# Moving weight sums, a transpose and a tail between engines in a decoder layer on eight cores

## The reference

```python
hcat = x @ w_in                          # B, C, h (512 each) | q, k, v, g (512 each)
y_conv = B * causal_short_conv(C * h, conv_w)            # 3 taps, depthwise
q, k = rotary(q), rotary(k) * 128 ** -0.5
o = chunkwise_retention(q, k, v)         # 4 heads of 128, decay, running state
y_ret = silu(g) * head_group_norm(o)
mix = concat([y_conv, y_ret]) @ w_out
x = layer_norm(alpha * x + mix)
ff = square(relu(x @ w_ff1)) @ w_ff2     # 1024 -> 4096 -> 1024
ple = sigmoid(x @ w_ple_gate) * (p @ w_ple_proj)
x = layer_norm(alpha * x + ff + ple)
```

## Time and profile before

| | us |
|---|---|
| median of 6 runs | 953.4 (946.37 to 958.29) |
| profiled execution | 950.21 |
| span of its slowest core (core 0) | 948.7 |
| spans of the other cores | 894.7 to 948.6 |
| PE busy on core 0 | 783.1 (83%) |
| DVE busy | 579.7 (61%) |
| ACT busy | 226.3 (24%) |
| POOL busy | 162.7 (17%) |

### The profile page before, as it was taken

How to read it: one execution, slowest core, us unless ns; L and a number is a source line. 1 busy time by engine, 2 the same in 40 slices (tenths; PEclk the granted TensorE clock), 3 DMA queues, 4 the chain that set the end, 5 groups by cost and what they waited for, 6 DMA issues and landing times.

```text
span 948.7 us, 12219 instructions; the slowest of 8 cores (894.7 to 948.7 us)
## 1 busy us (share of the span) xinstructions
PE 783.1 (83%) x3864; PEld 362.2 (38%) x3864; DVE 579.7 (61%) x832; ACT 226.3 (24%) x456; POOL 162.7 (17%) x208
## 2 busy tenths in 40 slices
PE   4999958788878973899999999800699999999980
PEld 1444424444434421344444444300244444444430
DVE  4558756559987692566447773200376766657697
ACT  2222234443454201344332000000033333200000
POOL 8000235434545311001000000000011110000011
PEclk9999989999999986899999999955799999999995
DMA  9992665687456996957321345995547553234112
GB/s 128 163 212 39 103 152 124 140 179 160 114 122 133 252 191 135 242 126 162 114 89 45 133 170 96 146 56 42 109 97 172 163 187 120 90 133 168 55 66 111
DMA packets 54207, 124.20 MB, mean 131 GB/s; under 512 B 16000, under 2 KB 32512, under 8 KB 47232
## 3 DMA queue, kind: packets, MB, share of 16 engines
q0 software_dynamic: 13248, 51.91, 31.8%
q1 hardware_dynamic: 39744, 69.42, 27.1%
q10 hardware_dynamic: 1152, 2.10, 0.6%
HBM read 133.37 MB, written 30.41 MB: 173 GB/s over the span
## 4 chain that ended last, share of the span: by engine, by line
PE 57%; DMA 13%; DVE 10%; issue 5%; SPq 5%; POOL 4%; another core or an unknown queue 4%; ACT 2%; DVEq 0%; POOLq 0%; ACTq 0%
PE ps L178 56%; SPq L220 5%; DVE xacc L196 3%; DMA ycat<-s_x 3%; DMA s_x<-x1b_54 3%; DMA stg_122<-w_ff 2%; DMA xT_56<-xT 2%; DMA s_op<-stg_121 1%; DMA stg_121<-w_ff 1%; DVE xacc L185 1%; POOL st_51 L185 1%; DVE lnst L987 1%; DVE stg_121 L185 1%; ACT sqj L207 1%
## 5 line engine op out<-in xcount | busy, mean ns | idle before, releaser
L185 DVE TENSOR_TENSOR xacc<-xacc,ps 128x512 f32<-128x512 f32 x96 | 63.7, 684 | 129.5 <-PE ps L178 127.8
L178 PE MATMUL ps<-ycat,ring_106 128*128 128x512 bf16 x256 | 60.5, 400 | 19.1 <-DMA ycat<-s_x 17.0
L207 ACT ACTIVATE tR_129<-ps 128x512 f32<-128x512 f32 x43 | 25.6, 596 | 199.6 <-PE ps L178 193.0
L185 POOL TENSOR_TENSOR lnst<-lnst,neghalf 128x1 f32<-128x1 f32 x32 | 23.8, 745 | 268.9 <-DVE lnst L189 268.8
L178 PE MATMUL ps<-ring_104,ycat 128*128 128x512 bf16 x256 | 60.7, 387 | 5.3 <-DVE xtmp L196 5.2
L178 PE MATMUL ps<-ring_105,hT 128*128 128x512 bf16 x64 | 15.8, 409 | 58.1 <-DMA ring_105<-s_op 58.1
L178 PE MATMUL ps<-ring_105,ycat 128*128 128x512 bf16 x256 | 60.2, 384 | 0.5 <-DVE xtmp L196 0.5
L185 DVE TENSOR_TENSOR hT<-ps,tR_127 128x512 bf16<-128x512 f32 x43 | 29.6, 689 | 48.4 <-ACT tR_127 L207 47.3
L178 PE MATMUL ps<-ycat,ring_107 128*128 128x512 bf16 x256 | 55.9, 379 | 0.0
L178 PE MATMUL ps<-ring_109,ycat 128*128 128x512 bf16 x224 | 51.9, 379 | 0.0
L178 PE MATMUL ps<-ring_108,ycat 128*128 128x512 bf16 x224 | 51.9, 379 | 0.0
(11 more groups left out here) (262 smaller groups left out, 1419.9 us busy)
## 6 DMA issues: line engine op xcount, KB each, us to landing
s_op<-stg_121 SPq DMA_DIRECT2D x8, 896.0 KB, 6.2
s_op<-stg_122 SPq DMA_DIRECT2D x8, 896.0 KB, 9.3
ring_104<-s_op SPq DMA_DIRECT2D x6, 1024.0 KB, 4.8
ring_105<-s_op SPq DMA_DIRECT2D x6, 1024.0 KB, 5.0
stg_121<-w_ff POOLq DMA_DIRECT2D x8, 512.0 KB, 6.6
stg_122<-w_ff POOLq DMA_DIRECT2D x8, 512.0 KB, 5.6
xtmp<-x SPq DMA_DIRECT2D x8, 512.0 KB, 12.9
ring_106<-w_ff POOLq DMA_DIRECT2D x4, 1024.0 KB, 11.5
```

Source lines behind the costliest of these rows:

```text
L178: self.P.op("pe", lambda e: e.matmul(out, lhsT=lhsT, rhs=rhs, start=start, stop=stop, skip_group_check=skip), reads, writes)
L185: self.P.op(eng, lambda e: e.tensor_tensor(out=out, in0=in0, in1=in1, op=op), reads, writes)
L207: self.P.op("act", lambda e: e.activation(out=out, in_=in_, func=func, **kw), reads, writes)
```

## The change

- **Staging.** Five buffers in place of two. Pieces 0 to 5 are loaded right after the other weights; their sums run on GpSimd, written ahead of the convolution. Their buffers 0 and 1 lie where the retention's `qr`, `kr`, `vb`, `qkT`, `PT` and `Sb` will be, buffer 2 on the rotary scratch. Pieces 6 to 13 stay in the retention on DVE, loaded at even t and summed at odd t, in buffers 3 and 4. Pieces 14 and 15 are loaded after the loop and summed on GpSimd in the projection. The output projection's slabs are asked for at t = 3 in place of before the loop.
- **`s_op`** is laid out by piece: the store has runs of 7 KB, a slab load runs of 1 KB in place of 8 KB.
- **Tile 1** is transposed by PE, with an ACT cast and copy for each block, in the projection's blocks 12 to 15; the LayerNorms of tiles 2 and 3 both go to the first ff1.
- **Transposing loads** of tiles 2 and 3 are issued by ACT; the second of a tile writes a name of its own (`x1T`), which the matmuls of ff1 and gate read as well.
- **Second half's order** is M1, M2, M5, M3, M4, M6, M7; the sums for M6 and M7 run on GpSimd, written ahead of M5 and of M3.
- **Tail.** For all blocks but block 3: scale and shift to mean 0 on ACT, the weight on DVE, the bias on GpSimd, one output DMA on SP's queue.

```diff
-ORDER = (("M1", "M2", "M5", "M6", "M7", "M3", "M4"), ("M1", "M3", "M2", "M4", "M5", "M6", "M7"))
+ORDER = (("M1", "M2", "M5", "M6", "M7", "M3", "M4"), ("M1", "M2", "M5", "M3", "M4", "M6", "M7"))
...
-    s_op = nc.dram_tensor("s_op", [7, 2, 128, 8, 512], BF16).ap()
+    s_op = nc.dram_tensor("s_op", [16, 128, 7, 512], BF16).ap()
...
-    stg = [at("stg%d" % i, [128, 7, 512], BF16, (o_wc + 16 * KB, o_tR)[i], ("stg", i))
-           for i in range(2)]
+    stg = [at("stg%d" % i, [128, 7, 512], BF16, off, ("stg", i))
+           for i, off in enumerate((o_rb, o_rb + 7 * KB, o_rt, o_tR, o_wc + 16 * KB))]
+    STG = [0, 1, 2, 3, 0, 1] + [3, 4] * 5
...
-                    h.dma("sp", ring[i][:], s_op[PRODS[nm][0], g], ("ringh", i),
-                          [("s_op", g * 8 + c) for c in range(8)],
+                    h.dma("sp", ring[i][:],
+                          s_op[g * 8:g * 8 + 8, :, PRODS[nm][0], :].rearrange("c p n -> p c n"),
+                          ("ringh", i), [("s_op", g * 8 + c) for c in range(8)],
                           [("ring", i)])
...
+        def gen_piece(c, eng):
+            i = STG[c]
+            t, r = stg[i], [("stg", i)]
+            h.tt(eng, t[:, 4, :], t[:, 0, :], t[:, 3, :], ALU.add, r, r)
             yield
+            h.tt(eng, t[:, 5:7, :], t[:, 1:3, :][:, ::-1, :], t[:, 0:4:3, :], ALU.subtract, r, r)
             yield
+            h.tt(eng, t[:, 1:3, :], t[:, 1:3, :], t[:, 0:4:3, :], ALU.add, r, r)
+            h.dma("sp", s_op[c], t[:], ("stgst", i), r, [("s_op", c)])
             yield
...
+        for c in range(4):
+            piece_load(c)
+        for c in range(6):
+            for _ in gen_piece(c, "pool"):
+                pass
+            if c >= 2 and c + 2 < 6:
+                piece_load(c + 2)
+
         conv((0, 0), by_piece=True)
...
-        piece_load(0)
-        prefetch(2)
-        piece_load(1)
...
-                h.dma("sp", ycat[:, a, 4 * k:4 * k + 4, :], s_x1[tt, :, k * 512:(k + 1) * 512],
-                      ("x1tr", k), [("s_x1", 4 * tt + b) for b in range(4)], ycr(a),
-                      transpose=True)
+                h.dma("act", ycat[:, a, 4 * k:4 * k + 4, :], s_x1[tt, :, k * 512:(k + 1) * 512],
+                      ("x1tr", a, k), [("s_x1", 4 * tt + b) for b in range(4)],
+                      ycr(a) if k == 0 else [("x1T", a)], transpose=True)
...
-            if t < NB:
-                pieces.add(gen_piece(t))
+            if t % 2 == 0 and t < NB:
+                piece_load(6 + t // 2)
+            elif t < NB:
+                pieces.add(gen_piece(6 + t // 2, "dve"))
...
-            if t >= 1:
-                piece_load(t + 1)
...
+            if t == 3:
+                prefetch(2)
...
         pieces.flush()
-        bg.add(gen_norm1(1))
-        prefetch(6)
+        piece_load(14)
+        piece_load(15)
+        for b in range(4, 8):
+            chains.append(gen_ln1(b))
+            bg.add(chains[b])
+        prefetch(5)
         for b in range(8, 16):
             for hf in range(2):
                 mix_part(b, hf, wo[hf][0], wo[hf][1], next_bank())
                 bg.step(3)
             if b == 11:
-                bg.flush()
-                x1_load_T(1)
-                bg.add(gen_norm1(2))
-        bg.add(gen_norm1(3))
+                for c in (14, 15):
+                    for _ in gen_piece(c, "pool"):
+                        pass
+            if b >= 12:
+                bg.until(chains[b - 8])
+                x1_cast(b - 8)
+                x1_transpose(b - 8)
+        for tt in (2, 3):
+            bg.add(gen_norm1(tt))
...
+                if n == 0:
                     bg.add_first(hsum("M2"))
-                if m in nxt:
-                    bg.add_first(hsum(nxt[m]))
+                if m == "M2":
+                    bg.add_first(hsum("M5"))
+                if m == "M5" and last:
+                    for _ in hsum("M6", "pool"):
+                        pass
+                if m == "M3" and last:
+                    for _ in hsum("M7", "pool"):
+                        pass
+                if m in ("M5", "M6") and not last:
+                    bg.add_first(hsum({"M5": "M6", "M6": "M7"}[m]))
...
+            if b != 3:
+                nb = lnst[:, b, 15:16]
+                h.stt(nb, mv[:, 0:1], -1.0, rstd, ALU.mult, ALU.mult, [rl, ("rstd", b)], [("nb", b)])
+                h.act(buf, buf, AF.Identity, [rb, ("rstd", b), ("nb", b)], [rb], scale=rstd, bias=nb)
+                yield
+                h.tt("dve", buf, buf, lnt[2][:], ALU.mult, [rb, "ln2w"], [rb])
+                yield
+                h.tt("pool", buf, buf, lnt[3][:], ALU.add, [rb, "ln2b"], [rb])
+                h.dma("sp", out[ob_ * 128:(ob_ + 1) * 128, :], buf, ("outl", b, 0), [rb],
+                      [("out", ob_, 0)])
```

More of the change, by code:

```diff
@@ L460, in piece_load @@
             if c < 16:
[L461 to L465, removed]
+                i = STG[c]
+                cast(stg[i][:, 0:4, :], w_ff2[c], ("stg", i), ("stg", i))
+        def gen_piece(c, eng):
+            i = STG[c]
+            t, r = stg[i], [("stg", i)]
+            h.tt(eng, t[:, 4, :], t[:, 0, :], t[:, 3, :], ALU.add, r, r)
             yield
-            h.tt("dve", t[:, 5:7, :], t[:, 1:3, :][:, ::-1, :], t[:, 0:4:3, :], ALU.subtract, r, r)
+            h.tt(eng, t[:, 5:7, :], t[:, 1:3, :][:, ::-1, :], t[:, 0:4:3, :], ALU.subtract, r, r)
             yield
-            h.tt("dve", t[:, 1:3, :], t[:, 1:3, :], t[:, 0:4:3, :], ALU.add, r, r)
-            h.dma("sp", s_op[:, c // 8, :, c % 8, :].rearrange("m p n -> p m n"), t[:],
-                  ("stgst", c % 2), r, [("s_op", c)])
+            h.tt(eng, t[:, 1:3, :], t[:, 1:3, :], t[:, 0:4:3, :], ALU.add, r, r)
+            h.dma("sp", s_op[c], t[:], ("stgst", i), r, [("s_op", c)])
             yield
@@ L878, in phase_ff1 @@
                             h.mm(ps[bank][:], slab[:, kc, f * 128:(f + 1) * 128],
-                                 ycat[:, a, kc, :], kc == 0, kc == 7, [rs] + ycr(a), [RP[bank]])
+                                 ycat[:, a, kc, :], kc == 0, kc == 7,
+                                 [rs, ("x1T", a)] + ycr(a), [RP[bank]])
                         i = rn[0] % 3
@@ L898, in phase_gate @@
                         h.mm(ps[bank][:], ycat[:, b // 4, kc, ck(b)], slab[:, kc, :],
-                             kc == 0, kc == 7, ycr(b // 4) + [rs], [RP[bank]])
+                             kc == 0, kc == 7, ycr(b // 4) + [rs, ("x1T", b // 4)], [RP[bank]])
                     h.act(sg[i][:], ps[bank][:], AF.Sigmoid, [RP[bank]], [("sg", i)])
@@ L922, in hv, with hsum @@
                     [("hT", fh * 16 + c, a) for c in range(c0, c1)])
-        def hsum(m):
+        def hsum(m, eng="dve"):
             ba, bb, sign = PRODS[m][1]
@@ L928, in hsum @@
                 (va, ra_), (vb_, rb_) = hv(ba, c, c + 4), hv(bb, c, c + 4)
-                h.tt("dve", dst[:, c:c + 4, :], va, vb_, ALU.add if sign > 0 else ALU.subtract,
+                h.tt(eng, dst[:, c:c + 4, :], va, vb_, ALU.add if sign > 0 else ALU.subtract,
                      ra_ + rb_, rd)
@@ L949, in phase_ff2 @@
             for n, m in enumerate(order):
-                nxt = {"M2": "M5", "M5": "M6", "M6": "M7"} if not last else {
-                    "M3": "M2", "M2": "M5", "M4": "M6", "M6": "M7"}
-                if n == 0 and not last:
+                if n == 0:
                     bg.add_first(hsum("M2"))
-                if m in nxt:
-                    bg.add_first(hsum(nxt[m]))
+                if m == "M2":
[8 more added lines that the diff above has]
+                    bg.add_first(hsum({"M5": "M6", "M6": "M7"}[m]))
                 two = [None, None]
@@ L974, in phase_ff2 @@
                             ff2_add(4 * a + p, hf, bank, sign)
-                        if last and m == "M5":
+                        if last and m == "M3":
                             last_stats(p, 1)
+                        if last and m == "M4":
+                            last_stats(4 + p, 0)
                         if last and m == "M6":
-                            last_stats(4 + p, 0)
                             bg.add(gen_last(4 + p, 1))
@@ L1001, in gen_last @@
             yield
+            ob_ = 8 + b
+            if b != 3:
[8 more added lines that the diff above has]
+                      [("out", ob_, 0)])
+                outs.append(("out", ob_, 0))
+                yield
+                return
             halves = [(buf[:, k * 512:(k + 1) * 512], (rb, "half", k)) for k in range(2)]
@@ L1007, in gen_last @@
                 yield
-            ob_ = 8 + b
             for k in range(2):
```

## The result

The kernel after takes 928.1 us (median of 10 runs, 921.6 to 935.5), the kernel before 954.05 in the same comparison (20 runs); the ratio is 0.973, its 95% interval 0.969 to 0.977. It is faster, by 26 us; the forecast was 59 us, to 894.

What follows compares the result with a forecast made beforehand. PE was taken to set the pace, so its waits count. From the slowest core's span: 948.7 + 10 - 20 - 17 - 3 - 33 + 4 = 889.7; with 1.5 and 3.2, 894 us, range 858 to 936.

Steps and rivals of the forecast that it cites:

- Between, nearer core 0 since the slowest core counts: 25.: Second ff1: PE's new wait for a transposed tile, replacing the 58 us slab wait; 25 us, bounds 0 to 40.
- -33: Products: transposing loads on ACT remove the 58 us slab wait but bring a 25 us tile wait; net -33 us.
- So it profits where loads are quick: Products: the fourth transposing load, starting right behind the third, gains where loads are quick; part of the 25 us wait.
- As late as before: Rival, chance 0.18: the fourth transposing load lands at +88.5 us on the slowest core; wait 40, time 909 us.
- The crawl: Rival, chance 0.08: third and fourth transposing loads take 72 us each, one after the other; wait 105, time 974 us.
- Retention start +10: Retention start: GpSimd's weight sums delay the first qkT copy about 18 us; net +10 us, bounds -2 to +40.
- iterations -20: Retention loop: fewer sums on VectorE and no load waiting for the previous store; -20 us, bounds -8 to -30.
- GpSimd and VectorE hold each other up: Rival, chance 0.12: at the start GpSimd's sums take twice as long, the start slips by 40 us; time 934 us.
- Tile 1 by TensorE -17: Output projection and first ff1: the 17.0 us tile wait and slow clock go, 2.5 us of PE work comes; -17 us.
- The flush +4: First ff1, slab 4: 24 LayerNorm steps left, 15 us of VectorE before the relu products, partly covered; about +4 us.
- Product sums hidden, tail +4: M6 and M7 sums on GpSimd hidden; last LayerNorm's chain 6.1 us a block for 3.8; +4 us, bounds -4 to +9.
- Slabs with runs of 1 KB at nothing: Products: slab loads in 1 KB runs cost nothing while asked for five slabs ahead; otherwise 34 us for a layer.

Runs made afterwards that it cites:

- e1: Kernel after, with the second ff1's casting loads issued during M7, M3 and M4 held until all four transposing loads have landed; 870.45 us, lowest of four.
- e11: Kernel after, with each casting load issued during M7, M3 and M4 cut into eight (1 KB runs), nothing held back; lowest time 883 us.
- e7: Kernel of e1 without the 18 GpSimd sums of pieces 0 to 5, so it computes something else; 857.3 and 860.4 us.
- e5: Kernel after with e1's held casting loads and the LayerNorm of tiles 2 and 3 spread over the first ff1, no flush; 856.8 and 857.9 us, ratio 0.912.

## Why the prediction was right or wrong

- **The step that failed: "Between, nearer core 0 since the slowest core counts: 25."** The wait that takes the place of the 58 us was bounded by 0 and 40 and measured 54.5 on the slowest core, 18 on the best; -33 became -3.8. The direction (the transposed tile is late next, because it meets the casting loads) was right, the size was not, and the bounds were wrong too. They were the landings of the fourth load on cores 1 and 0 of before, 39 and 88 us after M6's end; after the change it landed at 66 to 102. "So it profits where loads are quick" came out the other way round. The packets tell something of why. Core 1 of before, from 584 to 588, then core 0, from 600 to 604 (SP's transposing loads are in q1, the casts in q0):

```profile
q1 hardware_dynamic: 1847, 0.47, 89.1%
q0 software_dynamic: 42, 0.31, 37.1%
...
q0 software_dynamic: 90, 0.74, 101.9%
q1 hardware_dynamic: 90, 0.02, 3.8%
```

On core 1 the transposing load burst through a gap: from 586 to 587, between the packets of one casting load and those of the next, it moved 1134 packets beside none. On core 0 there was no gap. Core 1's first five casting loads took 10 to 16 us; after the change the last three took 22 to 62, by core, and the last transposing load landed only as they ended. That the waits between the loads on SP had left core 1's casting loads time to finish is argued from these counts, not shown; only the remedy (e1, e11) was run.
- **The rivals.** "As late as before" (909, wait 40) was nearest: its direction, with too small a wait. The crawl (974) was not reached; its reason against, that only a few casting loads are outstanding until PE goes on, is what ended the wait.
- **Retention start +10, iterations -20.** The first qkT copy came 19.4 us later on the slowest core (forecast 18), the sums cost 10 to 13 by e7. The wait of 8.5 that was set against it did not go: kr still waited 9.4 us, with the load order slabs before piece now the other way round. From the first qkT copy to the last transposes of `ob` PE took 175.3 us in place of 205.1, so the iterations gave -29.8, at the edge of the bounds; from there to the first ff1 35.6 in place of 39.3, -3.8 (forecast -7.8 + 2.5; waits for xtmp of 5.4 stayed of the 7.8). To the first ff1 the forecast adds up to -15.3 (10 - 20 - 7.8 + 2.5), measured -14.1: the sum is near by luck, since two misses of some 10 us cancel.
- **GpSimd and VectorE hold each other up.** This rival (chance 0.12, 40 us) came true in part: on VectorE's side, for some eight multiply-adds, while a piece's sums took GpSimd 5.7 to 6.9 us (forecast 6.8). The Trainium skill's page "GPSIMD Engine Reference", section "Key points", names VectorE instructions with two SBUF inputs: the rows of e7 and after agree (748 against 2560 ns, the product from PSUM 692 in both).
- **Tile 1 by TensorE -17.** Right: the wait is gone, and the slow group with it.
- **The flush +4.** Measured 11.2 + 1.6 by PE's rows, 13.6 by e5. Mis-sized: a block has eight steps, not seven, so four blocks were left in place of 3.4, and each took 5.0 us in place of 4.4, 0.5 to 0.6 of it a wait of the second multiply-add for pow:

```profile
404.45 1.28 DVE L196 SCALAR_TENSOR_TENSOR xtmp<-xtmp,lnst,ln1b 128x1024 f32<-128x1024 f32 x1 [0.59 <-POOL lnst L185]
409.41 1.28 DVE L196 SCALAR_TENSOR_TENSOR xtmp<-xtmp,lnst,ln1b 128x1024 f32<-128x1024 f32 x1 [0.51 <-POOL lnst L185]
414.43 1.28 DVE L196 SCALAR_TENSOR_TENSOR xtmp<-xtmp,lnst,ln1b 128x1024 f32<-128x1024 f32 x1 [0.58 <-POOL lnst L185]
```

- **Product sums hidden, tail +4.** Hidden, though a 128x2048 sum took 4.06 us in place of the 5.4 forecast; the tail came out at +2.4, a block at 5.97 us (forecast 6.1).
- **Slabs with runs of 1 KB at nothing.** Right: no PE wait for a slab from s_op on the slowest core.

The 35 us of span between forecast and measurement are then: the tile 29.2 (33 - 3.8), the flush about 9, less some 3 from the other terms.

Open: the stretches in which the transposing packets are slow as such (core 2 from 588 to 656 and core 4 from 570 to 588 in the kernel after; core 0 of before from 612 to 660, 1468 packets beside 264 casting ones). Much of the 54.5 us falls in them: core 4, with a short one, waited 18. Which cores are slow changes from run to run; with casts in runs of 4 KB the waits were shorter, and in runs of 1 KB none was left. What these stretches are was not found.

## What to carry to other kernels

When a queue's wait is removed, ask what kept the waiting loads apart from other traffic: here the wait on SP seems to have left gaps in which a transposing load got through, and without it the last of four loads landed only when the casts had ended. Count packets per queue in a stretch of a few microseconds; a load of many small packets beside one of large packets moved here at the large one's packet rate at times (93 beside 92), and held both up at others. So let the small ones go first and hold the large ones until they have landed, 16 us in e1. And price each edit of a part by itself: the tail's two edits, -6.6 and +9, looked like one of +2.4.

## What was unexpected of the hardware

- Beside casting loads with 8 KB runs the transposing loads moved 0.02 MB in 4 us, without them 0.49; with casts in 1 KB runs 0.13.
- On core 2 of the kernel after, the granted clock from 600 to 655, of which PE worked the first 4.9 us and then idled, was 0.57 on average, so mostly at the lower level of 1.2 GHz, and over PE's first nine microseconds after it 0.81 (us, PE busy, then the other engines, clock, DMA):

```profile
600.00:655.00 55.00, 4.92 (x23) 2.06 (x21) 0.00 (x0) 0.02 (x1) 0.00 (x0) 0.57 1.21 60
659.00:668.00 9.00, 8.52 (x33) 3.61 (x35) 5.10 (x7) 1.79 (x3) 0.66 (x2) 0.81 0.01 2
```
